# One hybrid decoder layer with a mixture of experts on one core: w2 slices read with 8 KB per partition instead of two rows of 4 KB, and the activation written in the matching column order

## The reference, cut to what matters

```python
def clamped_swiglu(hu):
    x_glu, x_lin = hu[..., :D_FF], hu[..., D_FF:]
    x_glu = jnp.minimum(x_glu, SWIGLU_LIMIT)
    x_lin = jnp.clip(x_lin, -SWIGLU_LIMIT, SWIGLU_LIMIT)
    return x_glu * jax.nn.sigmoid(SWIGLU_ALPHA * x_glu) * (x_lin + 1.0)
...
        act = clamped_swiglu(xb @ w1[e] + b1[e])      # w1[e]: 1024 x 2048
        return act @ w2[e] + b2[e]                    # w2[e]: 1024 x 1024
```

## Time and profile before

| | us |
|---|---|
| runs | 1311.32, 1316.43, 1316.05; median 1316.05 |
| profiled execution, its own time | 1313.04 |
| its span, first to last instruction | 1311.3 |
| TensorE busy | 1208.0 (92%) |
| VectorE busy | 901.6 (69%) |
| ScalarE busy | 659.3 (50%) |
| GpSimd busy | 206.5 (16%) |
| moved by DMA | 454.33 MB |

### The profile page before, as it was taken

How to read it: one execution, slowest core, us unless ns; L and a number is a source line. 1 busy time by engine, 2 the same in 40 slices (tenths; PEclk the granted TensorE clock), 3 DMA queues, 4 the chain that set the end, 5 groups by cost and what they waited for, 6 DMA issues and landing times. The chain is left out here.

```text
span 1311.3 us, 14828 instructions
## 1 busy us (share of the span) xinstructions
PE 1208.0 (92%) x5626; PEld 852.8 (65%) x5626; DVE 901.6 (69%) x746; ACT 659.3 (50%) x631; POOL 206.5 (16%) x192
## 2 busy tenths in 40 slices
PE   5889989688999999999999999999999999999990
PEld 4667777567557677677577677577677577577630
DVE  4397765868367498488488579479579479579507
ACT  4324333464356376366366367357457357357312
POOL 5480000261110010110110110101211111111000
PEclk9989999688999999999999999999999999999996
DMA  6500351777999999999999999999999999999996
GB/s 242 199 13 1 129 208 65 302 267 293 410 417 416 418 417 416 417 411 416 409 405 413 409 404 417 401 413 402 411 400 416 402 411 406 406 396 417 414 391 258
DMA packets 93755, 454.33 MB, mean 346 GB/s; under 512 B 16072, under 2 KB 16104, under 8 KB 60818
## 3 DMA queue, kind: packets, MB, share of 16 engines
q1 hardware_dynamic: 84690, 434.15, 82.3%
q0 software_dynamic: 8416, 17.11, 3.4%
q10 hardware_dynamic: 576, 2.10, 0.4%
HBM read 445.56 MB, written 17.97 MB: 353 GB/s over the span
## 5 line engine op out<-in xcount | busy, mean ns | idle before, releaser
L1225 DVE TENSOR_TENSOR ring_lo<-ring,w_hi 128x2048 fp32r<-128x2048 f32 x240 | 542.5, 2290 | 133.9 <-ACT w_hi L1530 133.5
L1530 ACT ACTIVATE w_hi<-ring 128x2048 fp32r<-128x2048 f32 x240 | 457.7, 1917 | 229.5 <-DMA ring<-in_w 134.8
L762 PE MATMUL ps<-w_hi,blockT_hi 128*128 128x512 f32 x640 | 255.1, 399 | 5.3 <-DVE ring_lo L1225 5.3
L763 PE MATMUL ps<-ring_lo,blockT_hi 128*128 128x512 f32 x640 | 250.7, 392 | 0.0
L764 PE MATMUL ps<-w_hi,blockT_lo 128*128 128x512 f32 x640 | 250.3, 391 | 0.0
L779 PE MATMUL ps<-ring,blockT_raw 128*64 128x512 f32 x768 | 166.8, 592 | 0.0
L808 PE MATMUL ps<-w_hi,actT_hi 128*128 128x512 f32 x320 | 131.0, 410 | 15.0 <-DVE ring_lo L1225 14.9
L762 PEld LDWEIGHTS ps<-w_hi,blockT_hi 128*128 128x128 f32 x640 | 121.3, 190 | 33.0 <-DVE ring_lo L1225 5.7
L764 PEld LDWEIGHTS ps<-w_hi,blockT_lo 128*128 128x128 f32 x640 | 121.1, 189 | 25.5
L763 PEld LDWEIGHTS ps<-ring_lo,blockT_hi 128*128 128x128 f32 x640 | 121.2, 189 | 25.1
L810 PE MATMUL ps<-w_hi,actT_lo 128*128 128x512 f32 x320 | 126.5, 395 | 0.0
(11 more groups left out here) (262 smaller groups left out, 1339.1 us busy)
## 6 DMA issues: line engine op xcount, KB each, us to landing
ring<-in_w SPq DMA_DIRECT2D x384, 1024.0 KB, 20.3
ring<-in_w_in SPq DMA_DIRECT2D x12, 768.0 KB, 10.8
ring<-expert_rows SPq DMA_DIRECT2D x16, 512.0 KB, 14.9
X<-in_x SPq DMA_DIRECT2D x8, 512.0 KB, 6.1
ring<-in_w_out SPq DMA_DIRECT2D x8, 512.0 KB, 4.1
h_rows<-normed ACTq DMA_DIRECT2D x4, 512.0 KB, 2.7
out<-ring SPq DMA_DIRECT2D x4, 512.0 KB, 2.6
ring<-in_b SPq DMA_DIRECT2D x3, 256.0 KB, 8.7
```

Of the source, the lines that this page charges most:

```text
L762: mm(ps[:, c, :], x_hi, high[:, cols], start=False, stop=False)
L763: mm(ps[:, c, :], x_hi, ring_lo[:, r, cols], start=False, stop=False)
L1225: v.tensor_tensor(ring_lo[:, r, :], ring[:, r, :], w_hi[buffer].bitcast(F32), ALU.subtract).then_inc(lo_ready, 1)
L1530: a.activation(w_hi[buffer], ring[:, r, :], ACT.Copy).then_inc(hi_ready, 1)
```

## The change

A slot of w2 still holds the same 256 rows, but partition p now takes the neighbouring rows 2p and 2p + 1 of the slice, which are 8 KB in one piece. So block k of a slice (k = 0, 1) now holds the rows with remainder k instead of the k-th half. The activation's columns have to follow: `activated` reads its inputs in order and writes element (s, q, k) to column s*256 + k*128 + q, so that two elements that follow each other go to places 128 elements (512 bytes) apart. The overflow part uses the same two functions.

```diff
             def load_w2(e, k, r):
 
-                src = w2[0, e].rearrange("(s k p) n -> p s k n", p=P, k=W2_K)
-                sp.dma_start(ring[:, r, :].rearrange("p (k n) -> p k n", k=W2_K), src[:, k, :, :]).then_inc(slot_in[r], 16)
+                src = w2[0, e].rearrange("(s p k) n -> p s (k n)", p=P, k=W2_K)
+                sp.dma_start(ring[:, r, :], src[:, k, :]).then_inc(slot_in[r], 16)
...
-                v.tensor_tensor(width(act_v, big), width(lin_c, big), width(sig, big), ALU.mult).then_inc(actv_ready, 1)
+                turned, a_in, b_in = width(act_v, big), width(lin_c, big), width(sig, big)
+                v.tensor_tensor(turned.rearrange("p (s k q) -> p s q k", k=W2_K, q=P), a_in.rearrange("p (s q k) -> p s q k", k=W2_K, q=P),
+                                b_in.rearrange("p (s q k) -> p s q k", k=W2_K, q=P), ALU.mult).then_inc(actv_ready, 1)
```

## The result

The changed kernel takes 1305.24 us in the median of six runs (1304.49 to 1311.23), the kernel before 1315.74 beside it. The ratio, which weighs all runs of both, is 0.9934 with a 95% interval from 0.9914 to 0.9955: faster by 0.66%, 8.7 us, and beyond what the measurement is uncertain by. The two medians lie further apart, by 10.5 us. The profiled execution took 1304.65 us over a span of 1302.9.

A forecast was written before the change was run, and what follows sets the result against it. The prediction took the DMA engines, whose queue never empties, to bound the expert part. 8KB rows give 8.8 us off, queue and activation write 0: 1316.05 - 8.8, about 1307 us, range 1290 to 1318.

The forecast's parts named there:

- The bound: Expert part: a DMA queue that never empties sets the period, 97.1 us a triple; TensorE needs 2.0 to 2.8 us less.
- the landing time of 20 us: w1 and w2 loads land some 20 us after issue, a slot alone takes about 2.5: some eight of twelve slots always queued.
- Part 1: w2 loads in rows of 8 KB instead of 4 KB: 0.073 us saved per slot, 120 slots, 8.8 us off; bounds 0 and 12.
- the last products gain with the rest: Small experts' last second products: TensorE waits six times for a slot, 3.8 us together, and these shrink too.
- Part 2: SyncE's queue: half the descriptors per w2 issue, stalls of about 4 us shrink or go; costed at nothing behind the 20 us backlog.
- rival A: TensorE's floor, about 1291 us: packets and issue stalls cost the DMA engines more than counted, TensorE's waits go; chance 0.18.
- the share of 0.51: Deepest dip, 1160 to 1162 us, 209 GB/s: read as half the DMA engines idle because scatters and gathers load them unevenly.
- Part 3: VectorE's hopping activation write: 2.1 us for a big expert, 0.9 more, 23 us of work altogether; cost 0, covered by slack.
- B: Packets don't matter, 1316 us: the 2.7 to 3.3% rate differences come from what else ran; chance 0.26 together with D.
- C: Slower, about 1324 us: a write above 2.7 ns an element delays VectorE's first low part of the next w1; chance 0.09.
- D: The queue's hardware still cuts 8 KB into the former pieces, so nothing happens; chance 0.26 together with B.

## Why the prediction was right, point by point

**The bound.** The prediction held that the DMA engines set the pace and that a saving on them comes through although TensorE is busy 98% of the stretch. The runs without gathers show it from the other side: as soon as the engines have less to do, 10 us of difference between the two loads shrink to 1.8. But the row on which the prediction rested most, the landing time of 20 us, doesn't show it by itself. With 4 KB pieces and no gathers it is still 16.5 us, and TensorE sets the pace; with four slots in flight it is 10.4 us, and TensorE still has gaps (busy for 737.93 of the 750 us). TensorE's waits tell the two cases apart.

**Part 1, 8.8 us.** The change gave 8.7 us by the ratio and 8.4 between the profiled executions. The term was 0.073 us a slot; w1 in 4 KB pieces measured 0.074, and the single pieces give 0.07 to 0.10. For w2 a triple gained 1.23 us over 12 slots, 0.10 each, more than the term. With six or four slots in flight 0.84 us of that remain, 0.070 a slot.

That the total came out so close is in part luck, by parts that cancel. The eight triples of the earlier trace rows gave 9.8 us where the term gives 7.0. But the first of their clamps stands 1.5 us later than before, at 401.58, and after the last of them only 0.2 us more are won. Half of the late start is there before any w2 load is issued: TensorE's first matmul of the experts starts at 252.56 us where it was 251.78, and the first load of w2 is issued at 268.6. The same clamp stands at 399.76 us in the kernel with six slots in flight and at 404.89 in the one with the write alone, so this part moves by some us from one execution to the next. Behind the close hit stand two misses of 2 to 3 us, of opposite sign.

To the second belongs a sentence of the forecast, that the last products gain with the rest. The small experts' second products waited for a slot 2.9 us in five places, not 3.8 in six (the sixth wait, 0.8 us, was for ScalarE), and they wait 2.8 us in five after the change:

```profile
PE ps L825 <- DMA ring<-in_w: 2.8, 5, 0.9
```

The rule of the Trainium skill that was weighed here ("DMA: Bandwidth & Descriptors", section Specifications: line rate from 512 bytes on) doesn't hold to the last 3%: a slot takes 2.54, 2.47 and 2.44 us in pieces of 4, 8 and 16 KB. By that rule the kernels with pieces of 4, 8 and 16 KB would all have taken the same time. The same page of the Trainium skill, section Bandwidth, names a small fixed overhead per packet for small descriptors; a price of that kind, some 10 ns a piece by the records above, fits what is seen at 4 KB and 8 KB still.

**Part 2, costed at nothing.** The stalls went, as forecast: 3.93 us before, 0.91 us at most after. Their worth was put at 0. If the limit of six or four loads is a fair stand-in for them, it is 0.3 to 0.4 us a triple, 2 to 4 us over the kernel; that is not shown. Two things speak for less: w1 in 4 KB pieces stalled harder than the kernel before and cost what the pieces alone explain, and in the rows above the last of the eight loads goes out 27 us behind the second product's bias with the stall and without it, since the queue waits for used slots anyway. Either way it is the smaller part and not rival A, whose price was 25 us. The dips of the earlier trace rows got shallower, too: the lowest 1 us stretch after 600 us is now

```profile
727.00:728.00 1.00, 1.00 (x6) 0.83 (x5) 1.00 (x1) 0.00 (x0) 0.00 (x0) 1.00 0.89 283
```

with 283 GB/s where one with 205 stood, a half of the earlier trace rows. But the kernel with w1 in 16 KB, in which no issue takes over 0.48 us, has a dip as deep as before, so the stalls are not what makes them:

```profile
1159.00:1160.00 1.00, 1.00 (x6) 0.84 (x5) 0.00 (x0) 0.00 (x0) 0.00 (x0) 1.00 0.48 205
```

That the scatters and gathers load the engines unevenly, and the loaded ones set the pace, was argued from the share of 0.51 and was not tried by itself; the runs without gathers show that their bytes matter, not on which engines.

**Part 3, costed at nothing.** 2.03 us was measured for 2.1 forecast, 1.09 us for the small form where half of 2.1 was said, and the first low part ends some 0.7 us before TensorE's first matmul, where 1.5 less 0.9 was left (the two low parts in the first row end 2.2 us apart):

```profile
408.18 4.49 DVE L1225 TENSOR_TENSOR ring_lo<-ring,w_hi 128x2048 fp32r<-128x2048 f32 x2
```

```profile
411.16 0.58 PE L762 MATMUL ps<-w_hi,blockT_hi 128*128 128x512 f32 x1
```

The write alone: ratio 1.0005. The row of the reduction that hops 512 bytes at every read was a good stand-in for a write that does. The page "Vector Engine (DVE) Microarchitecture Reference" of the Trainium skill, section Measured stream behaviour on trn2, gives 1.71 ns a column for a hop of 4 KiB at each write, 1.8 us by an estimate; the 512-byte hop here measured 2.03, so the nearest row of the trace was the better guide.

**The rivals.** A (TensorE's floor, 1291) is not what the change reaches but what lies behind it: without gathers both kernels stand on it, at 1286 to 1288. B (packets don't matter) falls with the load alone, which has the whole gain, and with the 4 KB w1, which loses it. C (VectorE late for the next w1) needed a write slower than 2.7 ns an element; it is 1.98. D is excluded by the count of packets.

## What to carry to other kernels

Don't take a reader that is busy 98% of the time for the one that sets the pace: look at what its few waits are for. If they are for loads that were issued long before and landed late, the DMA engines set the pace, and 2 or 3% off each of these loads comes through until the waits are used up. A landing time of many times a load's own is a hint, no proof: it was 16.5 us in a kernel at TensorE's floor. Then make the contiguous piece per partition as long as the layout lets you, and pay for the new row order where an operand is turned by TensorE anyway; a transpose that reads every second or fourth column takes 293 ns where it took 281. What bounds it is the next engine's floor, which a run with part of the traffic left out shows. Here it is 94.13 us a triple. With 40 transposes a triple at 12 ns more it is about 94.6, an estimate, and four triples of the kernel with everything in 16 KB take 94.65 to 94.68 us.

## What was not expected of the hardware

- Loads still get faster beyond 4 KB per piece: a piece takes 159 ns at 4 KB, 309 at 8 KB and 611 at 16 KB, so one piece less saves 9 ns and then 7.
- TensorE's floor doesn't show in the DMA engines' share: it is 1.01 and 1.02 there, as in the kernels in which TensorE waits for loads.
- An issue on SyncE's queue can take up to 7.8 us with two pieces per partition everywhere, median 0.65 us; with one it takes 0.33 and never over 0.91. Holding the queue to four slots in flight costs no more than holding it to six: 96.24 and 96.25 us a triple.
- Taking 1.8% of the bytes off the DMA engines (8.4 of 454 MB) took 1.5% off the time (1305.2 to 1285.8 us).
